# Two MoE layers whose expert weights stream in over one queue: the down weights of an expert are put in front of the gate and up weights of the next

## The reference, cut to what matters

```python
y = jnp.zeros_like(h)
for e in range(N_EXPERTS):                                  # 16 experts, D = 1024, EXPERT_FF = 256
    he = jax.nn.silu(h @ w_gate[e]) * (h @ w_up[e])
    y = y + comb[:, e:e + 1] * (he @ w_down[e])             # comb: 0 except for a token's two experts
```

## Time and profile before

| what | value |
|---|---|
| median of three runs | 1218.99 us (1208.46 to 1221.63) |
| profiled execution, and its span | 1216.92 us, 1215.1 us |
| TensorE matmuls busy | 1101.6 us, 91% of the span |
| VectorE, ScalarE, GpSimd busy | 70%, 40%, 17% |
| expert stage of layer 0 (222 to 498.5 us) | 276.5 us for 24 slots |
| expert stage of layer 1 (952 to 1197.2 us) | 245.2 us for 22 slots |
| granted TensorE clock in these two stages | 0.96 of full speed in each |
| share of time that the 16 DMA engines are busy in them | 0.80 and 0.76 |

### The profile page before, as it was taken

The page is one execution under the profiler, slowest core; times in us unless marked ns, Lnnn a source line. Parts: engine busy times, 40 slices in busy tenths (PEclk is TensorE's granted clock), DMA queues, the critical chain, the costliest instruction groups (busy, mean ns, idle before and its releaser), DMA issues.

```text
span 1215.1 us, 16407 instructions
## 1 busy us (share of the span) xinstructions
PE 1101.6 (91%) x4737; PEld 813.6 (67%) x4738; DVE 850.8 (70%) x991; ACT 491.1 (40%) x679; POOL 206.8 (17%) x138
## 2 busy tenths in 40 slices
PE   5899898799889899879999999999998799889994
PEld 2554356666667677647888888878886677667762
DVE  5896997688988698565444444463667788688884
ACT  5210223465556566541111111141123466467663
POOL 2100120323233234200000000000000133223341
PEclk9989998799999999889999999999998699989997
DMA  9859236478987987612732233322225668978852
GB/s 350 344 211 397 120 120 244 163 268 243 346 272 235 311 255 225 186 58 74 286 102 93 104 121 121 121 75 100 89 119 208 232 201 275 327 271 297 270 127 40
DMA packets 83531, 243.03 MB, mean 200 GB/s; under 512 B 10576, under 2 KB 35352, under 8 KB 75292
## 3 DMA queue, kind: packets, MB, share of 16 engines
q1 hardware_dynamic: 61252, 180.48, 39.4%
q0 software_dynamic: 18496, 48.32, 15.6%
q10 hardware_dynamic: 3736, 13.65, 3.0%
HBM read 220.39 MB, written 40.89 MB: 215 GB/s over the span
## 4 chain that ended last, share of the span: by engine, by line
PE 62%; DVE 16%; DMA 9%; issue 5%; ACT 3%; DVEq 1%; ACTq 1%; SPq 1%; POOL 0%; POOLq 0%
PE PS L1853 16%; PE PS L1755 7%; PE PS L1957 7%; PE PS L1961 7%; PE PS L1958 7%; PE PS L1866 5%; DMA RAW<-in_moe_w_up_dram 4%; DVE ACC L1074 4%; PE PS L1872 4%; PE PS L1843 3%; PE PS L1610 3%; DVE H L1212 1%; DMA WAE<-in_w_ada_dram 1%; DVE WL L1390 1%; ACT WH L851 1%
## 5 line engine op out<-in xcount | busy, mean ns | idle before, releaser
L1390 DVE TENSOR_TENSOR WL<-RAW,WH 128x1024 fp32r<-128x1024 f32 x204 | 240.0, 1220 | 37.2 <-ACT WH L851 36.7
L851 ACT ACTIVATE WH<-RAW 128x1024 fp32r x196 | 196.5, 1055 | 51.8 <-DMA RAW<-in_moe_w_up_dram 45.0
L1853 PE MATMUL PS<-WH,XTH 128*128 128x512 f32 x384 | 159.8, 416 | 19.7 <-DVE XTL L1383 10.8
L1957 PE MATMUL PS<-HTH,WINH 128*128 128x512 f32 x384 | 150.8, 393 | 6.1 <-DVE HTL L1511 5.8
L1853 PE MATMUL PS<-WL,XTH 128*128 128x512 f32 x384 | 155.1, 404 | 0.0
L1853 PE MATMUL PS<-WH,XTL 128*128 128x512 f32 x384 | 154.9, 403 | 0.0
L1958 PE MATMUL PS<-HTL,WINH 128*128 128x512 f32 x384 | 149.9, 390 | 0.0
L1961 PE MATMUL PS<-HTH,WINL 128*128 128x512 f32 x384 | 118.7, 390 | 0.0
L1853 PEld LDWEIGHTS PS<-WH,XTH 128*128 128x128 f32 x384 | 75.2, 196 | 39.2 <-issue 24.4
L1074 DVE SCALAR_TENSOR_TENSOR ACC<-WA,SC,ACC 128x1024 f32 (+1 forms) x72 | 92.3, 1282 | 12.4 <-DMA WA<-in_w_ada_dram 8.3
L1866 PE MATMUL PS<-WDR,HETF 128*128 x184 | 90.2, 614 | 10.9 <-DVE YO L1404 10.9
(11 more groups left out here) (234 smaller groups left out, 1763.3 us busy)
## 6 DMA issues: line engine op xcount, KB each, us to landing
RAW<-in_moe_w_gate_dram SPq DMA_DIRECT2D x32, 1024.0 KB
RAW<-in_moe_w_up_dram SPq DMA_DIRECT2D x32, 1024.0 KB
WDR<-in_moe_w_down_dram SPq DMA_DIRECT2D x32, 1024.0 KB
WA<-in_w_ada_dram SPq DMA_DIRECT2D x28, 1024.0 KB, 6.8
WAE<-in_w_ada_dram SPq DMA_DIRECT2D x12, 1024.0 KB, 8.8
WINR<-in_conv_w_in_dram SPq DMA_DIRECT2D x24, 512.0 KB, 3.9
WA<-in_w_ada_dram ACTq DMA_DIRECT2D x8, 1024.0 KB, 10.1
X<-x_dram SPq DMA_DIRECT2D x16, 512.0 KB, 5.1
```

What stands on the lines that cost most here:

```text
L851: nc.scalar.activation(piece_of(WH[par], i), raw_piece(e, i), ACT.Copy).then_inc(w_high, 1)
L1390: V.tensor_tensor(piece_of(WL[par], i), raw_piece(e, i), piece_of(WH[par], i).bitcast(f32), ALU.subtract).then_inc(w_low, 1)
L1853: ins = T.matmul(bank(2), x[:, ch, :], w[par][:, :, ch, :], start=ch == 0 and i == 0, stop=ch == NC - 1 and i == 2)
L1957: T.matmul(bank(b), WINH[par][:, ch, :], HTH[:, ch, cols], start=ch == 0, stop=False)
```

## The change

For both layers the queue's order is turned round. Down 1 is issued right after the routing, without a wait, ahead of gate/up 2. From then on the down weights of expert e-1, with their wait for expert e-3's last down product, stand in front of the gate and up weights of expert e, with their wait for the split of expert e-2's. No load, no buffer and no condition on any single load is changed, only the order of the waits and issues on SyncE.

```diff
             def after_down(e):
                 sp.wait_ge(yd_mm, end_of(e) + b)
 
+            load_down(layer, 1, 1)
             after_split(0)
             load_gate_up(layer, 2, 0)
-            load_down(layer, 1, 1)
+            after_down(0)
+            load_down(layer, 2, 0)
             after_split(1)
             load_gate_up(layer, 3, 1)
-            after_down(0)
-            load_down(layer, 2, 0)
             with sp.Fori(2, HALF) as j:
                 for k in range(2):
+                    after_down(2 * j + (k - 3))
+                    load_down(layer, 2 * j + (k - 1), 1 - k)
                     after_split(2 * j + (k - 2))
                     load_gate_up(layer, 2 * j + k, k)
-                    after_down(2 * j + (k - 3))
-                    load_down(layer, 2 * j + (k - 1), 1 - k)
             after_down(EXPERTS - 3)
             load_down(layer, EXPERTS - 1, 1)
```

## The result

The changed kernel takes 1356.66 us (median of four runs, 1354.88 to 1368.1) against 1217.7 us before (also four runs, one more than in the table above); the ratio is 1.1186, with a 95% interval of 1.1144 to 1.1227. It is slower by 139 us, where 1364 us had been forecast (range 1310 to 1405). The two profiled spans differ by 1356.0 - 1215.1 = 140.9 us, and all of that, to within 1 us, lies in the two expert stages.

The account below looks back on a forecast made before the run. The prediction took late weight loads, 45.0 us of ScalarE waits, and plain slots of 9.7 us with TensorE busy throughout; 106.5 + 33.0 + 5.1 = 144.6 on 1216.9 gave 1361.5, with 2.1 for the median 1364 us, range 1310 to 1405.

Parts of the forecast that it names:

- the ring: Closed loop at 1+1 slots: Y, load, split, YO, down product, next Y; the next load isn't issued before; 23.6 us a step.
- the three classes: Experts by their two predecessors' slots: 1+1 leaves one slot (9.7 us), 1+2 or 2+1 two (19.4), 2+2 three (29, no cost).
- The nine 1+1 steps: Experts 6, 10, 11, 12 of layer 0 and 6, 7, 8, 9, 15 of layer 1: 216.5 us for 110.0, loss 106.5.
- T: From issue of the down and gate/up pair to its use: 8.0 loads + 1.9 gathers/scatters + 3.4 rest = 13.3 us.
- tail: From ScalarE's use of the load to the next Y, read at the next issue: 10.3 us with TensorE cold, 8.7 warm.
- The two-slot places: Eleven experts with 1+2 or 2+1 slots before them: seven lose 3.9 us each, together with experts 13 and 5 33.0 us.
- the 23.3 us: Time a load with its tail takes at a two-slot place, against 19.4 us for two plain slots: 3.9 us lost each.
- After a stall: First slot after a stall is 1.7 us over 9.7; new after experts 15 of layer 0, 3 and 12 of layer 1: 5.1.
- B: Rival: closed loop, loads nearly alone on the DMA engines, T 10.0, tail 9.5, a step 19.5 us: 1313 us; chance 0.22.
- D: Rival: hidden anyway, one-slot stretches bound by the DMA engines at 11.8 us a slot, about 1219 us, no change; chance 0.03.
- E: Rival: faster, down weights in front take away late down loads, at most 6 us back, 1213 us; chance 0.02.
- Y: End of a slot's down product; ScalarE was forecast to arrive 2 us before it, with nine waits of 13 to 16 us.

Follow-up runs that it names:

- x3: Queue order turned round only at the six experts whose two predecessors have 2+2 slots, against the kernel before: 1212.9 us against 1217.0, ratio 0.998.
- x4: Queue order turned round only at the nine experts whose two predecessors have 1+1 slots, against the kernel before: 1313.4 us, ratio 1.083.
- x5: Queue order turned round only at the eleven experts with 1+2 or 2+1 slots before them, against the kernel before: 1246.1 us, ratio 1.025.
- x2: Kernel before with gate/up e also waiting for expert e-3's down product, but still issued in front of down e-1: 1294.6 us, ratio 1.066.
- x6: Changed kernel with all four weight pieces of slot s+1 split in round s by ScalarE and VectorE: 1278.8 us, ratio 1.054 to the kernel before.
- x9: Changed kernel with the gate and up loads of experts 2 to 15 cut to half, result not the reference's: 1305.7 us, a single execution.
- x1: Kernel before with only down 1 moved in front of gate and up 2, in both layers: 1214.0 us against 1214.5, ratio 1.001.
- x12: Kernel before with all four weight pieces of slot s+1 split in round s by ScalarE and VectorE: 1200.2 us against 1213.1, ratio 0.989.
- x10: Kernel before with gate/up e issued in front of down e-2 and its wait where expert e-2 has one slot: 1207.2 us against 1214.5, ratio 0.994.
- x11: Kernel before with the alterations of x12 and x10 together: 1212.0 us, ratio 0.998.
- x8: Changed kernel with six more matmuls in every slot between the token transposes and the wait for the YO tile: 1464.7 us, a single execution.

## Why the prediction was right, step by step

**The mechanism** was read rightly: which wait moves, the ring it closes, and that it goes by the slots of two neighbouring experts. x3, x4 and x5 confirm the three classes, x2 that it is the wait in the main (78 of 139 us without the transfer in front), and x6 that ScalarE's and VectorE's order carries a good part of it.

**The nine 1+1 steps.** Forecast 216.5 us for 110.0, a loss of 106.5; measured from down product to down product 208.9 for 110.2, a loss of 98.7. The loss was thus oversized by 8 us. T was 12.0 us in the eight ordinary steps (forecast 13.3). The 8.0 us of the loads was right, 8.2 in the rows beside x9; the 1.9 us for gathers and scatters and the 3.4 for the rest make 5.3 where 3.7 was measured, and which of the two was too large stays open. The tail was 11.0 us in the same eight (forecast 10.3), since the clock stays down longer into the down product: the six products of line 1872 take 1.4 to 2.5 us in the eight steps, 2.1 on average, where the two cold cases before had 1.39 and 1.41. The two errors nearly cancel, 23.1 a step for 23.6, which is luck. Expert 6 of layer 0 took 24.2, not 27.7; the 2.6 us for the WA load in T was wrong, T being 11.1 there, while its tail was 13.1 for 11.8.

**The two-slot places.** Forecast +33 us, measured +46.8 together. The seven at 3.9 each measured +7.9 and +6.9 (experts 9 and 15 of layer 0), +6.0, +6.8, +7.9, +1.4 and +7.0 (3, 5, 10, 12, 14 of layer 1). Experts 13 and 5 of layer 0, forecast at 2.7 and 3.0, measured +3.3 and +2.5. The failed term is the 23.3 us, taken from the lowest span before, which had a warm tail of 8.7 us. SyncE's and ScalarE's rows of the changed kernel for expert 5 of layer 1:

```profile
1071.00 0.38 SPq L459 DMA_DIRECT2D WDR<-in_moe_w_down_dram  x1
...
1085.56 2.01 ACT L851 ACTIVATE WH<-RAW 128x1024 fp32r x2 [7.09 <-DMA RAW<-in_moe_w_up_dram]
```

The pair was issued from 1071.00 on and the next down load at 1097.08, so T is 14.6 and the tail 11.5 us, 26.1 together. Of the DMA engines' time from 1071 to 1086 us the gathers and scatters take 0.361*15 = 5.4 us, where it was 1.0 in the ring:

```profile
q1 hardware_dynamic: 560, 3.15, 51.8%
q0 software_dynamic: 533, 1.21, 36.1%
```

So the load is contended here, and TensorE runs its four products in 3.77 us, cold again, after 3.56 us without work. Expert 7 of layer 0 gained 2.8 us where nothing was forecast.

**After a stall** 5.1 us were forecast at three places; measured are 0, 0.5 and 2.0, together 2.5. The start gives back 5.5 us, and x1 and x5 show that the start varies like that without the change. With small differences the rest of the sum is -4.6 us. All together 98.7 + 46.8 - 4.6 = 140.9. The forecast had 106.5 + 33.0 + 5.1 = 144.6, so its terms were off by 8 us too much, 14 too little and 10 too much. That the sum is within 4 us is luck; that it is near 140 and goes by the places with little room is not.

**The rivals.** B, loads nearly alone, was nearly right on the neighbours, 1.0 to 2.2 us of engine time for the 3.8 of a slot, but had the rest of T at 2.0 where 3.7 was measured, and the tail at 9.5 for 11.0. D, hidden anyway, is refuted by the DMA share of 0.00 in the ring. E, that early down weights help, came true in its small part: ScalarE's 6.0 us of waits for them are gone. No gain shows from it, and the gate and up loads set the pace.

**What was to be seen.** The issue distance of 1.5 to 2 us was 1.3 to 1.9 from expert 4 on; waits of 150 to 200 us were 214.3. The nine of the 1+1 steps are 14.4 to 17.6 us long, where 13 to 16 were forecast (ScalarE arrives 3 to 5 us before Y and not 2), and eleven others make up 65.6 us. The steps of about 23 us are there. Finally, the clock in the stages was to lie under 0.96 and is 0.88 and 0.86:

```profile
222.00:560.00 338.00, 270.08 (x1088) 195.53 (x1088) 234.69 (x238) 164.82 (x225) 81.73 (x50) 0.88 0.66 211
1013.00:1338.00 325.00, 247.32 (x1000) 180.26 (x1000) 198.36 (x205) 152.40 (x208) 77.07 (x45) 0.86 0.59 184
```

## What to carry to other kernels

On a queue with blocking waits, the order of the waits can cost more than that of the transfers: the wait alone made 78 of the 139 us here (x2). Before turning two loads round, write down for each what its wait is for and how many steps lie between that event and the first use of every load behind it. Then look whether the engine that uses the load stands, in its own order, in front of the event that releases the next one; if so the delay isn't paid once but closes a ring in which nothing overlaps. For a load that is late now and then, try using it later on the engine before issuing it earlier: here the first gained 1.1% (x12) and the second 0.6% (x10), and both together nothing (x11).

## What the runs showed of the hardware that was not expected

The cost of a late load is not in proportion to its lateness. Putting the 1 MB behind instead of in front (x2) was worth 3.2 us at the 1+1 places and all the loss at two-slot places of layer 0. And a TensorE that has been idle for ten microseconds runs a down product in 4.8 to 6.3 us (the eight ordinary steps of the changed kernel) where a warm one needs 3.1, so such a wait costs two or three more behind it.

The Trainium skill (TensorE: Matmul & The Clock Gate, Why this matters for your kernels) warns of idle gaps between bursts of matmuls, since they bring back the slow clock. The trace agrees: granted clock 0.50 from 1107 to 1117 us. In x8 filling the gap only in part did not help: TensorE was busy 5.3 us longer, idle 4.81 us after that, and the clock was at 0.50 again for the down product.
